# The inner LayerNorms of a four-layer decoder step: statistics as rows, half of the mean's subtraction on GpSimd, and low parts between add-backs

## The reference

```
x <- layer_norm(alpha * x + mixer(x))          # alpha = (2 * 4) ** 0.25

def layer_norm(x, g, b):
    mu = mean(x, -1);  var = mean((x - mu) ** 2, -1)
    return (x - mu) * rsqrt(var + 1e-5) * g + b
```

## Time and profile before

| what | us |
|---|---|
| median of 3 executions | 1559.03 |
| the executions | 1549.67, 1559.03, 1560.87 |
| the profiled execution | 1562.84 |
| span of the profiled execution (first to last instruction) | 1561.1 |

### The profile page before, as it was taken

The page is one execution under the profiler, slowest core; times in us unless marked ns, Lnnn a source line. Parts: engine busy times, 40 slices in busy tenths (PEclk is TensorE's granted clock), DMA queues, the critical chain, the costliest instruction groups (busy, mean ns, idle before and its releaser), DMA issues.

```text
span 1561.1 us, 33329 instructions
## 1 busy us (share of the span) xinstructions
PE 1438.9 (92%) x12506; PEld 1310.9 (84%) x12506; DVE 969.4 (62%) x2096; ACT 727.4 (47%) x1414; POOL 609.9 (39%) x728
## 2 busy tenths in 40 slices
PE   8997989999999988878999999999998899799985
PEld 7996978888888866668989988988897699799885
DVE  5577562555564565536657877977977643646755
ACT  4676242444455344413445454544644422467721
POOL 4564532222212110156134544443544645256531
PEclk9998979999999998988789999999999799899987
DMA  5222343667667667522122323333432132223221
GB/s 158 77 73 56 89 122 116 191 198 233 205 211 224 213 204 213 155 68 67 34 70 71 109 75 110 109 86 85 112 109 86 57 107 86 79 72 87 72 59 58
DMA packets 282537, 179.72 MB, mean 115 GB/s; under 512 B 18906, under 2 KB 280826, under 8 KB 282376
## 3 DMA queue, kind: packets, MB, share of 16 engines
q1 hardware_dynamic: 282376, 177.58, 39.0%
HBM read 160.67 MB, written 16.86 MB: 114 GB/s over the span
## 4 chain that ended last, share of the span: by engine, by line
PE 57%; DVE 22%; ACT 7%; issue 7%; SPq 3%; POOL 3%; DMA 1%; DVEq 0%; ACTq 0%; POOLq 0%
PE proj L1839 8%; PE proj_lo L1839 7%; PE proj L198 6%; PE proj_lo L1070 5%; PE proj_lo L198 5%; PE proj L1070 4%; DVE conv L2341 3%; PE r L1081 3%; PE x L1165 2%; PE s L1126 2%; POOL w_low L173 1%; DVE m L2370 1%; DVE m L2386 1%; DVE h L686 1%; PE s L1093 1%
## 5 line engine op out<-in xcount | busy, mean ns | idle before, releaser
L173 POOL TENSOR_TENSOR w_low<-w_raw,w_high 128x256 fp32r<-128x256 f32 x608 | 528.0, 899 | 852.5 <-ACT w_high L164 852.5
L164 ACT ACTIVATE w_high<-w_raw 128x1024 fp32r<-128x1024 f32 x152 | 160.4, 1055 | 142.9 <-PE proj_lo L1839 51.1
L1839 PE MATMUL proj<-xh,w_high 128*128 128x288 f32 x440 | 137.9, 313 | 3.4 <-POOL w_low L173 2.2
L1839 PE MATMUL proj<-xh,w_low 128*128 128x288 f32 x440 | 132.6, 301 | 0.0
L1839 PE MATMUL proj<-xl,w_high 128*128 128x288 f32 x440 | 132.4, 301 | 0.0
L1839 PE MATMUL proj_lo<-xh,w_high 128*128 128x256 f32 x440 | 129.4, 294 | 0.0
L1839 PE MATMUL proj_lo<-xl,w_high 128*128 128x256 f32 x440 | 126.3, 287 | 0.0
L1839 PE MATMUL proj_lo<-xh,w_low 128*128 128x256 f32 x440 | 125.5, 285 | 0.0
L1839 PEld LDWEIGHTS proj_lo<-xh,w_high 128*128 128x128 f32 x440 | 85.5, 194 | 10.2 <-issue 10.2
L1839 PEld LDWEIGHTS proj<-xh,w_high 128*128 128x128 f32 x440 | 86.2, 196 | 7.3 <-POOL w_low L173 3.7
L1839 PEld LDWEIGHTS proj<-xh,w_low 128*128 128x128 f32 x440 | 86.0, 195 | 0.0
(11 more groups left out here) (487 smaller groups left out, 4350.6 us busy)
## 6 DMA issues: line engine op xcount, KB each, us to landing
k_pages<-in_cache_k SPq DMA_DIRECT2D x256, 128.0 KB, 2.7
v_pages<-in_cache_v SPq DMA_DIRECT2D x256, 128.0 KB, 2.4
w_raw<-in_c_in_w SPq DMA_DIRECT2D x48, 512.0 KB, 4.0
w_raw<-in_a_in_w SPq DMA_DIRECT2D x32, 512.0 KB, 3.9
w_raw<-in_b_in_w SPq DMA_DIRECT2D x32, 512.0 KB, 4.4
w_raw<-in_a_out_w SPq DMA_DIRECT2D x16, 512.0 KB, 4.1
st<-in_state_ssd_h SPq DMA_DIRECT2D x16, 512.0 KB, 5.1
out_ssd_h_sample<-st SPq DMA_DIRECT2D x16, 512.0 KB, 5.7
```

Source lines behind the costliest of these rows:

```text
L164: act.activation(k.wh[par][:], k.raw[par][:], ACT.Copy).then_inc(k.sem["w_hi"], 1)
L173: step = pool.tensor_tensor(k.wl[par][:, tiles, :], k.raw[par][:, tiles, :], k.wh[par][:, tiles, :], ALU.subtract)
L1839: mm = pe.matmul(out, w[par][:, i, :], x[:, i, cols], start=first and opens and i == 0 and n == 0, stop=last and i == KT - 1 and n == 2, s ...
```

## The change

The three inner norms are written anew, and two orders are changed with them.

- `ln_tensor` makes mean and mean square as rows on all partitions, per column part (`k.r`; `k.x` and `proj_lo`), with no token columns and no turning back. Then it issues filler products (`keep_busy`, 4 + 3 + 5 + 4 of 128 x 512 into a `proj` bank that is overwritten later), each group behind a semaphore of the norm.
- `ln_scalar` squares the mean's row, copies it to SBUF (`k.sq[1]`), and makes the inverse as exp(-0.5 ln(var + eps)), which lands in `k.s`; the table of Ln and Exp is asked for at the start of `out_scalar`. The split of slot 1's weights stands after the second tile's `xh`. `xT` + bias is written later (`kept`), after layers 1 and 2 alone, and what reads it waits for `ln_kept`.
- `ln_vector` takes the mean off tiles 0 to 3 only; `ln_pool`, new, takes it off tiles 4 to 7 on GpSimd in two operations, from the SBUF copy. It stands in POOL's queue before the low parts of slot 1, in layers 1 and 2 behind the constants. `low` is (xT + bias) - xh in one operation.
- `multiply_new_x` makes the high half of slot 1 too, two tiles behind slot 0; the later code of slot 1 leaves that half out.
- `b_pool` puts one slot's low part behind each of the add-backs 1, 2, 4, 5 and 6.

SP's code is the same.

```diff
 def multiply_new_x(pe, k, s, use, layer):
-    multiply_as_made(pe, k, s, use, k.xh, k.xl, "x_tile", [(KT * (layer - 1) + i + 1, (i,)) for i in range(KT)])
+    def products(par, out, i, cols): ...
+    def next_high(i):
+        if i == 0:
+            pe.wait_ge(k.sem["w_lo"], s + 3)
+            pe.wait_ge(k.sem["p_evac1"], use // 2)
+        products(1, k.proj[:, 1, 0:T - HALF], i, slice(HALF, T))
...
+    for i in range(KT):
+        pe.wait_ge(k.sem["x_tile"], KT * (layer - 1) + i + 1)
+        products(0, k.proj[:, 0, 0:T - HALF], i, slice(HALF, T))
+        mm = products(0, k.proj_lo[:, 0:HALF], i, slice(0, HALF))
+        if i == KT - 1:
+            mm.then_inc(k.sem["pe_slot"], 1)
+        if i >= NEXT_BEHIND:              # NEXT_BEHIND = 2
+            next_high(i - NEXT_BEHIND)
+    for i in range(KT - NEXT_BEHIND, KT):
+        next_high(i)
+
+def keep_busy(pe, k, par, count):
+    for _ in range(count):
+        pe.matmul(k.proj[:, 1, :], k.wh[par][:, 0, :], k.wh[par][:, 0:4, :].rearrange("p a n -> p (a n)"), start=True, stop=True)
...
@@ a_pool, layer 3
     else:
+        ln_pool(pool, k, 2)
         low(1)
...
+BACK_THEN_LOW = (1, 2, 4, 5, 6)
@@ b_pool
+    ln_pool(pool, k, 0)
     low_parts(pool, k, SLOT_B + 1, 33)
...
         pool.tensor_tensor(k.xT[:, i, :], k.xh[:, i, :], k.xl[:, i, :], ALU.add).then_inc(sem["x_back"], 1)
-        if i == 1:
-            low_parts(pool, k, SLOT_B + 34, 1)
-    low_parts(pool, k, SLOT_B + 35, 6)
+        if i in BACK_THEN_LOW:
+            low_parts(pool, k, SLOT_B + 34 + BACK_THEN_LOW.index(i), 1)
+    low_parts(pool, k, SLOT_B + 34 + len(BACK_THEN_LOW), 7 - len(BACK_THEN_LOW))
@@ c_pool
     pool.memset(k.acc[:], 0.0).then_inc(sem["c_consts"], 1)
+    ln_pool(pool, k, 1)
@@ ln_tensor
+    if not last:
+        for part, cols in enumerate(LN_PARTS):      # (256 to 544, 0 to 256)
...
+            pe.matmul(mean_row(k, part), k.ones_d[:], sums[0][:, cols], start=True, stop=True)
+            pe.matmul(square_row(k, part), k.ones_d[:], sums[1][:, cols], start=True, stop=True).then_inc(sem["ln_half"], 1)
+        pe.wait_ge(sem["w_hi"], {0: SLOT_B, 1: SLOT_C, 2: SLOT_A[1]}[layer] + 1)
+        keep_busy(pe, k, 0, 4)
+        pe.wait_ge(sem["ln_vrow"], 2 * layer + 2)
+        keep_busy(pe, k, 0, 3)
+        pe.wait_ge(sem["ln_irow"], 2 * layer + 2)
+        keep_busy(pe, k, 0, 5)
+        pe.wait_ge(sem["ln_x"], each + 1)
+        keep_busy(pe, k, 0, 4)
+        return
@@ ln_scalar
+    def squared_mean(part, cols):
+        act.wait_ge(sem["ln_half"], 2 * layer + part + 1)
+        act.activation(k.sq[0][:, 0, cols], mean_row(k, part), ACT.Square).then_inc(sem["ln_msq"], 1)
+        act.activation(k.sq[1][:, 0, cols], mean_row(k, part), ACT.Copy).then_inc(sem["ln_mrow"], 1)
+    def inverse(part, cols):
+        act.wait_ge(sem["ln_vrow"], 2 * layer + part + 1)
+        chain_log = act.activation(k.sq[0][:, 1, cols], k.sq[0][:, 1, cols], ACT.Ln, bias=k.eps[:])
...
+        act.activation(row_of(k.s)[:, cols], k.sq[0][:, 1, cols], ACT.Exp, scale=-0.5).then_inc(sem["ln_irow"], 1)
...
     for i in range(KT):
         act.wait_ge(sem["ln_norm"], KT * layer + i + 1)
-        act.activation(k.xh[:, i, :], k.xT[:, i, :], ACT.Identity, bias=bias)
-        act.activation(k.xT[:, i, :], k.xT[:, i, :], ACT.Identity, bias=bias).then_inc(sem["ln_x"], 1)
+        act.activation(k.xh[:, i, :], k.xT[:, i, :], ACT.Identity,
+                       bias=k.par_m[:, i, 4 + layer:5 + layer]).then_inc(sem["ln_x"], 1)
+        if i == 1:
+            split_high(act, k, s, s // 2, 1)
+        if i > 2:
+            kept(i - 3)
@@ ln_vector
+    pieces = ((0, 4, high_cols), (0, 2, low_cols), (2, 2, low_cols))
...
+        if i >= len(needed):                        # needed = (2, 2, 3, 3)
+            dve.wait_ge(sem["ln_upper"], 2 * layer + 2)
...
-        dve.tensor_tensor(k.xl[:, i, :], k.xT[:, i, :], k.xh[:, i, :], ALU.subtract).then_inc(sem["x_tile"], 1)
+        dve.scalar_tensor_tensor(k.xl[:, i, :], k.xT[:, i, :], k.par_m[:, i, 4 + layer:5 + layer], k.xh[:, i, :],
+                                 ALU.add, ALU.subtract).then_inc(sem["x_tile"], 1)
...
+    variance(0, high_cols)
+    less_mean(0)
+    variance(1, low_cols)
+    less_mean(1)
+    dve.wait_ge(sem["ln_irow"], 2 * layer + 2)
+    scaled(0)
+    scaled(1)
+    less_mean(2)
+    low(0)
+    scaled(2)
+    low(1)
+    scaled(3)
+    low(2)
...
+def ln_pool(pool, k, layer):
+    upper = slice(KT // 2, KT)
+    for part, cols in enumerate(LN_PARTS):
+        pool.wait_ge(k.sem["ln_mrow"], 2 * layer + part + 1)
+        x = k.xT[:, upper, cols]
+        rows = k.sq[1][:, 0:1, cols].broadcast_to([P, KT // 2, cols.stop - cols.start])
+        pool.tensor_tensor(x, x, rows, ALU.subtract).then_inc(k.sem["ln_upper"], 1)
```

More of the change, by code:

```diff
@@ L1234, in b_tensor @@
             multiply_new_x(pe, k, s0, u0, 1)
-        elif p.slot is not None:
+        elif p.slot is not None and p.slot > 1:
             slot_half(p.slot, True)
@@ L2552, with mean_row, square_row @@
 SHIFT_TILES = 2
+LN_PARTS = (slice(HALF, T), slice(0, HALF))
+def mean_row(k, part):
+    return k.r[:, part, 0:LN_PARTS[part].stop - LN_PARTS[part].start]
+def square_row(k, part):
+    bank = k.proj_lo if part else k.x
+    return bank[:, 0:LN_PARTS[part].stop - LN_PARTS[part].start]
 def row_of(bank):
@@ L2639, in by_token @@
         return mm
-    for part, chunks, cols in ((1, (2, 3, 4), slice(HALF, SEQ)), (2, (0, 1), slice(0, HALF))):
+    for part, chunks in ((1, (2, 3, 4)), (2, (0, 1))):
         pe.wait_ge(sem["ln_sum"], each + KT - 2 + part)
@@ L2645, in ln_tensor @@
             mm = by_token(c)
[L2646 to L2649, removed]
     mm.then_inc(sem["ln_mean"], 1)
[L2651 to L2659, removed]
+    turn_tile(pe, k, KT - 1, range(CH))
 def square_tile(act, k, layer, m):
@@ L2687, in out_scalar @@
     last = layer == k.last
+    if not last:
+        act.preload_act_table_set("natural_log_exp_and_others")
     for n in range(ahead, KT + 1):
@@ L2699, in out_scalar, with x_kept @@
                 copy_turned(act, k, 2 * (n - 5) + 1)
+X_KEPT = ((), tuple(range(KT)), tuple(range(KT)))
+def x_kept(layer):
+    return sum(len(tiles) for tiles in X_KEPT[:layer])
 def ln_scalar(act, k, layer):
     sem = k.sem
[L2704 to L2707, removed]
     if layer == k.last:
+        for part, cols in enumerate(LN_PARTS):
+            square_last(act, k, layer, part, cols)
+        act.wait_ge(sem["ln_var"], 1)
+        act.activation(k.lns[:, 10:15], k.lns[:, 5:10], ACT.Sqrt, bias=k.eps[:]).then_inc(sem["ln_sd"], 1)
@@ new lines, in ln_scalar, with kept @@
+    square_last(act, k, layer, 0, LN_PARTS[0])
+    square_last(act, k, layer, 1, LN_PARTS[1])
+    for part, cols in enumerate(LN_PARTS):
+        squared_mean(part, cols)
+        inverse(part, cols)
+    s = (SLOT_B, SLOT_C, SLOT_A[1])[layer] + 1
+    def kept(i):
+        if i in X_KEPT[layer]:
+            act.wait_ge(sem["x_tile"], KT * layer + i + 1)
+            act.activation(k.xT[:, i, :], k.xT[:, i, :], ACT.Identity,
+                           bias=k.par_m[:, i, 4 + layer:5 + layer]).then_inc(sem["ln_kept"], 1)
@@ L2720, in centre @@
+        if i > 2:
+            kept(i - 3)
+    for i in range(KT - 3, KT):
+        kept(i)
 def centre(dve, k, layer, x, cols):
@@ L2792, in evacuate @@
             dve.wait_ge(k.sem["s_evac"], u + m + 1)
+    if layer == k.last:
+        dve.wait_ge(k.sem["ln_kept"], x_kept(layer))
     for m in range(KT):
@@ L2841, in y_rows @@
         step.then_inc(sem["y_made"], 1)
-    dve.wait_ge(sem["ln_mean"], layer + 1)
-    chain(dve.tensor_copy(k.lns[:, 0:CH], mean))
-    chain(dve.tensor_tensor(k.lns[:, 5:10], k.lns[:, 0:CH], k.lns[:, 0:CH], ALU.mult))
-    dve.tensor_tensor(k.lns[:, 5:10], square, k.lns[:, 5:10], ALU.subtract).then_inc(sem["ln_var"], 1)
     if last:
+        dve.wait_ge(sem["ln_mean"], 1)
+        chain(dve.tensor_copy(k.lns[:, 0:CH], mean))
+        chain(dve.tensor_tensor(k.lns[:, 5:10], k.lns[:, 0:CH], k.lns[:, 0:CH], ALU.mult))
+        dve.tensor_tensor(k.lns[:, 5:10], square, k.lns[:, 5:10], ALU.subtract).then_inc(sem["ln_var"], 1)
         dve.wait_ge(sem["y_params"], 32)
@@ L2850, in ln_vector @@
         y_rows(0, False)
-    else:
-        less_mean(0)
-    dve.wait_ge(sem["ln_sd"], layer + 1)
-    step = dve.reciprocal(k.lns[:, 15:20], k.lns[:, 10:15])
-    step.then_inc(sem["ln_inv"], 1)
-    if last:
-        dve.wait_ge(sem["ln_inv"], layer + 1)
+        dve.wait_ge(sem["ln_sd"], 1)
+        dve.reciprocal(k.lns[:, 15:20], k.lns[:, 10:15]).then_inc(sem["ln_inv"], 1)
+        dve.wait_ge(sem["ln_inv"], 1)
         y_rows(0, True)
```

74 lines of the change are left out of this document (52 added, 22 removed).

## The result

The changed kernel takes 1545.0 us in the median of 8 executions (1542.37 to 1548.51), the kernel before 1557.82 (1549.67 to 1563.22): ratio 0.9922, 95% interval 0.9905 to 0.994, 12.8 us less. The forecast was 1550 with 1540 to 1563. The profiled execution takes 1548.37 (span 1546.7), 14.5 less than that of before.

What follows compares the result with a forecast made beforehand. The prediction took TensorE to hold 57% of the path that sets the end, VectorE 22%. Its terms, 4.5 - 6.8 - 2 - 5 = -9.3, taken from 1559.03 gave a median of 1550 us, range 1540 to 1563.

Steps and rivals of the forecast that it cites:

- First norm, +4.5: First inner norm: scaling 3.85 earlier, but slot 3's load 4.65 later in SP's queue; 4.5 us slower, from +1.3 to +6.5.
- Rival (c): First norm: SP's queue does not decide, so the norm gives -6; total -19.8, 1539 us, chance 0.05.
- Output stage, -6.8: Attention layer's output stage: low parts between add-backs remove PE's 5.35 stop and 1.47 of clock; between -5.3 and -7.0.
- Third norm, -5: Third inner norm: GpSimd is free, slot 0's result comes at 1359.3 against 1364.23; -5 us, between -2 and -6.9.
- Second norm, -2: Second inner norm: PE waits for slot 1's weights, time-step products at 758.3 against 760.27; -2 us, between 0 and -5.
- The table load: Load for Ln, asked for in the output stage where ScalarE waits; between statistics and Ln it would cost 1.28 per norm.
- (a): Rival in the norms: the filler does not hold the clock; total -3.3, 1556 us, chance 0.22.
- The 3.5 of clock: First norm: slots 0 and 1 gain 3.5 us from a higher clock, if the filler holds it.
- (b): Rival in the norms: little contention, a low part loses only 0.5 to a GpSimd piece; -17.6, 1541 us, chance 0.13.
- The rule that I weighed: Norms: a VectorE instruction with two SBUF inputs is blocked until GpSimd's piece ends; first low part waits until 207.6.
- (d): Slower rival in the norms: GpSimd's subtractions at twice the price, 10.9 per norm; +4.8, 1564 us, chance 0.10.
- the -9.3 of the sum: Whole kernel: the four terms for three norms and output stage together, 4.5 - 6.8 - 2 - 5 us.

Runs made afterwards that it cites:

- e2: The changed kernel with SP reading page numbers one batch earlier, batch 1 before its wait for slot 3's load: 1539.47 us.
- e9: The changed kernel with SP reading page numbers of batches 0 and 1 ahead of slot 2's load, batch 2 ahead of slot 3's: 1535.00 us.
- e1: The changed kernel with the attention layer's add-backs in their old order (two adds, one slot's low part, six adds, six slots' low parts): 1553.45 us.
- e3: The changed kernel without the 16 filler products of each norm, their waits kept: 1549.16 us.
- e8: The changed kernel with GpSimd's subtraction and slot 1's low parts ahead of the state-space constants, and all engines' waits for these moved to first use: 1543.87 us.
- e5: The changed kernel with the table of exp and tanh asked for at the start of the attention layer: 1545.81 us.
- e6: The changed kernel with GpSimd's subtraction and slot 1's low parts ahead of the state-space constants, only PE's wait for these moved: 1547.86 us.

## Why the prediction was right, and where its steps were not

*First norm, +4.5: measured +3.5, and for the reason given.* The scaling came 3.96 sooner (3.85 forecast), GpSimd's pieces took 5.01 (5.45), the low part stood until they ended, and the whole gain vanished into SP's queue; e2 and e9 showed that, by taking the queue out. The sizes inside were off. Slot 1's low parts ended at 210.12, 10.45 behind the statistics' end, where the sum had 12.1 (212.5 less 200.41): the pieces ended 0.5 sooner, and the turns delayed VectorE's low parts (1.25 each) more than GpSimd's (3.78 for four). So slot 3's load went out 3.0 later, not 4.65, and the page transposes started 1.9 later, not 3.45; from there to the 24 products PE lost 1.6 to the low clock's slower work (transposes 1.94 for 1.09, the next 24 products 3.94 for 3.18), not 1. Slot 2's products, which the sum had 7.4 sooner, came 5.0 sooner (24.15 behind the last statistic's start, before 29.17). Rival (c), that SP does not decide, is refuted.

*Output stage, -6.8: measured -7.05*, with the stop and the low clock gone as described, and e1 giving it back.

*Third norm, -5: measured -4.9, partly by luck.* The scaling came 4.4 sooner (7.98 behind the statistic's start before, 3.57 after; forecast 3.85). GpSimd's pieces ended 5.2 behind the statistics' end (forecast 6.7), so that VectorE's first low part lost nothing to them (0.78) and ended 5.9 behind (forecast 7.4). What followed took as much longer: two low parts took 1.23 and 1.25 beside slot 1's low parts, which the sum had not counted in this norm, and from 1343.15 it was PE, with slot 1's products between the tiles, that ran without a break to the end, and not VectorE's thirteen operations. The clock has no share that shows: N3 is 18.74 in e3, 0.3 above the highest of the kernels with this code.

*Second norm, -2: the step that failed.* N2 is -4.0 and N2b -5.6. The sum had PE stand for slot 1's weights, due 15.9 behind the statistics (746.5 less 730.59). They came 14.3 behind (743.72 less 729.38), and PE did not wait for them: it waited 4.1 for VectorE's first two low parts and ran without a break from 742.49, 13.1 behind the statistics, 2.8 sooner than the sum had. That run took 12.6 to the time steps, 0.8 more than forecast (11.1 and 0.7). And the sum stopped at the time steps, while these and the slot behind them ran 1.6 shorter (0.54 and 1.01). What happened on GpSimd and VectorE was as described: pieces from the memset's end, low parts standing through them; e8 puts the price of that late start at 3.5.

*A term that was missing, +1.2.* The table load was costed at nothing in the output stage, which was right; what it leaves behind was not asked. Before, the layer's first exponential had ScalarE load the exp table behind the norm's root, at a time when ScalarE was idle (timeline of before):

```profile
222.87 1.28 ACT L1285 ACT_TABLE_LOAD   x1 [1.67 <-DVE lam L1401]
```

After, the table of ln and exp serves that exponential too, and the load falls on the first tanh, on the path: U1 +1.2, and e5 takes it back. The Trainium skill (ScalarE: Activation LUTs, "Table sets: the hidden batching unit") puts exp and tanh into one set and exp and ln into another; the trace agrees, with a load of 1.28 at the first tanh behind the ln set.

*The rivals.* (a) is half right and its price refuted: the granted clock was 1.00 in the first norm (201 to 216; before 0.52), 0.81 in the second and 0.90 in the third, where the forecast asked for above 0.9, and it fell to 0.50 and 0.61 where PE's own products set the pace; but without the filler the norms lost nothing. The 3.5 of clock that I had put into the first norm was not there either: slot 2's products start 24.85 behind the last statistic's start in e3, and 24.15 to 25.73 in after, e1, e5, e6 and e8. (b) asked for 0.5 per low part; they lost 1.2, 2.3 and 1.4. The rule that I weighed, that a two-input VectorE instruction is blocked until GpSimd's instruction ends, agrees with pieces of 2.4 to 2.9 us as with 0.7 us ones. (d) asked for pieces of 9.0; they take 5.0 to 5.5.

Against the terms, then: 3.6 us more in the second norm (-5.6 for -2), 1.0 in the first, 0.25 in the output stage, less 0.1 in the third and 1.2 for the table: 3.5 more than the -9.3 of the sum. The measured median lies 5 below the forecast, in a range 23 wide; most of the miss is the second norm.

## What to carry to other kernels

Follow a stage that is made faster to the queue that feeds what comes after it: here the first norm's gain was there for the taking, and 5.7 to 9.1 us of that stage came from moving register loads into a wait that SP had anyway. Before work goes to an idle engine, ask whose operands it blocks while it runs and what stands behind it in its own queue. And hold each part of a joined change against the kernel without it: each taken out alone, GpSimd's half and the filler brought nothing over the three norms together, and the thread 1.4 us.

## What the runs showed that I had not expected

A granted clock of 0.52 in place of 0.81 as a mean through a norm cost no time: while it differed VectorE set the pace, and where PE did it was 0.50 in both kernels. Cutting GpSimd's two subtractions into eight freed VectorE (1.22 for 3.03) and still lost 2.0 us in the first norm and 2.7 in the second. And the attention from the 24 products that stand at 372.69 in after to the start of Out took from 305.0 (e5) to 311.2 us (after), with the same code there, more than most of the terms above; only stages measured inside one trace could tell these apart.
